# Four seams of a hybrid encoder block in another order on VectorE, ScalarE and GpSimd

## What is computed

```
h = rmsnorm(x, g_mix); z = h @ w_in          # 1024 x 1792: lx, lg, q, k, v
y_lru = rmsnorm(rg_lru(conv(lx)) * gelu(lg), g_lru_out)     # recurrence, 512 channels
y_att = rmsnorm(chunk_window_attention(q, k, v, sinks), g_attn_out)   # 8 heads
x = x + concat([y_lru, y_att]) @ w_out
h = rmsnorm(x, g_ffn)
x = x + square(relu(h @ w_ff1)) @ w_ff2      # hidden width 4096
gate = sigmoid(rmsnorm(x, g_ple) @ w_ple_gate)
x = x + gate * (p @ w_ple_proj)
out = rmsnorm(x, g_final)
```

## Time and profile before

| | us |
|---|---|
| median of 3 runs (1131.03 to 1132.39) | 1131.92 |
| the profiled execution's own time | 1131.98 |
| its span, first to last instruction | 1130.2 |
| PE busy | 1081.9 (96%) |
| DVE busy | 742.2 (66%) |
| POOL busy | 519.3 (46%) |
| ACT busy | 435.3 (39%) |
| granted clock of TensorE, mean | 0.989 |

### The profile page before, as it was taken

The page is one execution under the profiler, slowest core; times in us unless marked ns, Lnnn a source line. Parts: engine busy times, 40 slices in busy tenths (PEclk is TensorE's granted clock), DMA queues, the critical chain, the costliest instruction groups (busy, mean ns, idle before and its releaser), DMA issues.

```text
span 1130.2 us, 13954 instructions
## 1 busy us (share of the span) xinstructions
PE 1081.9 (96%) x5016; PEld 880.7 (78%) x5016; DVE 742.2 (66%) x930; ACT 435.3 (39%) x749; POOL 519.3 (46%) x328
## 2 busy tenths in 40 slices
PE   7999999899989999999999999999999999899996
PEld 5778887676866788888888888888888888678995
DVE  6988639788789846536546545545654653885786
ACT  8554655454446123222222312312311322565455
POOL 2644262232205346256255344444534625565884
PEclk9999999899999999999999999999999999999998
DMA  7211102111001111210211111112111111412352
GB/s 280 75 38 38 38 1 85 38 38 38 1 1 38 54 59 38 74 37 37 74 37 37 74 37 68 44 37 74 37 47 64 37 74 50 173 38 75 111 166 98
DMA packets 22483, 69.45 MB, mean 61 GB/s; under 512 B 2352, under 2 KB 4400, under 8 KB 22448
## 3 DMA queue, kind: packets, MB, share of 16 engines
q1 hardware_dynamic: 22448, 68.99, 17.3%
HBM read 64.79 MB, written 4.19 MB: 61 GB/s over the span
## 4 chain that ended last, share of the span: by engine, by line
PE 77%; DVE 13%; ACT 4%; issue 4%; POOL 2%; DMA 1%; SPq 0%; DVEq 0%; ACTq 0%
PE bank L540 25%; PE bank L541 25%; PE bank L542 25%; DVE xT L1635 1%; DVE r_mix L1246 1%; DVE lane L1293 1%; POOL w_lo L426 1%; DVE acc L325 1%; POOL gx_lo L455 1%; DMA stage<-in_w_in 1%; PE bank L660 1%; PE bank L588 1%; DVE r_ffn L1246 1%; PE bank L630 1%; DVE pT_lo L1673 1%
## 5 line engine op out<-in xcount | busy, mean ns | idle before, releaser
L540 PE MATMUL bank<-h_hi,w_hi 128*128 128x512 f32 (+1 forms) x756 | 291.2, 385 | 18.3 <-DVE h_lo L1233 8.0
L542 PE MATMUL bank<-h_hi,w_lo 128*128 128x512 f32 (+1 forms) x756 | 284.2, 376 | 0.0
L541 PE MATMUL bank<-h_lo,w_hi 128*128 128x512 f32 (+1 forms) x756 | 284.2, 376 | 0.0
L1635 DVE TENSOR_TENSOR xT<-bank,xT 128x512 f32<-128x512 f32 x256 | 173.6, 688 | 114.1 <-PE bank L542 112.3
L540 PE MATMUL bank<-u_hi,w_hi 128*128 128x512 f32 x512 | 202.9, 396 | 7.5 <-DVE xT L1635 6.3
L542 PE MATMUL bank<-u_hi,w_lo 128*128 128x512 f32 x512 | 199.5, 390 | 0.0
L541 PE MATMUL bank<-u_lo,w_hi 128*128 128x512 f32 x512 | 199.4, 389 | 0.0
L540 PEld LDWEIGHTS bank<-h_hi,w_hi 128*128 128x128 f32 x756 | 145.0, 192 | 52.0 <-issue 13.9
L503 POOL TENSOR_TENSOR w_lo<-w_raw,w_hi 128x1024 fp32r<-128x1024 f32 x30 | 78.1, 2626 | 193.2 <-ACT w_hi L1120 193.2
L541 PEld LDWEIGHTS bank<-h_lo,w_hi 128*128 128x128 f32 x756 | 145.0, 192 | 26.1 <-issue 1.9
L542 PEld LDWEIGHTS bank<-h_hi,w_lo 128*128 128x128 f32 x756 | 144.6, 191 | 25.5
(11 more groups left out here) (202 smaller groups left out, 1717.2 us busy)
## 6 DMA issues: line engine op xcount, KB each, us to landing
w_raw<-in_w_ff SPq DMA_DIRECT2D x60, 512.0 KB, 3.6
stage<-in_w_ple_gate SPq DMA_DIRECT2D x24, 512.0 KB, 3.3
stage<-in_w_in SPq DMA_DIRECT2D x13, 512.0 KB, 3.5
stage<-in_w_out SPq DMA_DIRECT2D x8, 512.0 KB, 3.4
xT<-in_x SPq DMA_DIRECT2D x7, 512.0 KB, 9.0
stage<-in_w_ff SPq DMA_DIRECT2D x4, 512.0 KB, 3.2
out_x<-o_ring SPq DMA_DIRECT2D x4, 512.0 KB, 4.2
out_x<-o_ring SPq DMA_DIRECT2D x7, 256.0 KB, 2.2
```

What stands on the lines that cost most here:

```text
L540: pe.matmul(o, whi, hh, start=first, stop=False, skip_group_check=onto)
L541: pe.matmul(o, whi, hl, start=False, stop=False, skip_group_check=onto)
L542: return pe.matmul(o, wlo, hh, start=False, stop=last, skip_group_check=onto)
L1635: dve.tensor_tensor(dst, bank[4 + q % 4][:, :], dst, ALU.add).then_inc(y_added, 1)
```

## The change

No instruction is added or removed but for the place in the queue; one subtraction of weights (`low(2 * FF_FIRST + 3)`) moves from VectorE to GpSimd. The seams:

1. Recurrence norm: both `invert(SS_LRU..)` and both `norm_y` now stand at groups 22 to 24; `softmax_front(1)` stands ahead of `softmax_sum(0)`. ScalarE rounds piece 8 of the weights at unit 1 instead of ahead of unit 0.
2. End of attention: the sums of units 5 to 7 and two of the four multiplications of the attention norm's half 0 come after unit 7's copy of `probT`; PE's `sum_rows(SS_ATT + 1)` comes a group later, `add_a(1)` ahead of `invert`.
3. Start of the feed-forward: the root for half 1 comes between two roundings; `ffn_pair` of half 1 run in one piece, ahead of `rectify` and `hidden_low`; VectorE's `w_low` for one half of piece 12 comes ahead of the reciprocal, and the other half goes to GpSimd. PE's `sum_rows(SS_FFN + 1)` comes one k earlier.
4. End of the feed-forward: `embedding_high` follows the block's last two roundings, `sums(SS_PLE)` on GpSimd and `ple_high` on ScalarE stand ahead of the gate's first weight piece, and `pT_lo`, `pw_lo` come two adds later.

```diff
@@ gpsimd @@
+            low(2 * FF_FIRST + 3)
             pool.wait_ge(w_split, 2 * FF_FIRST + 4)
...
             w2_low(FF_BLOCKS - 1)
+            sums(SS_PLE, sq2, acc2)
             low(2 * GATE_FIRST)
             low(2 * GATE_FIRST + 1)
-            sums(SS_PLE, sq2, acc2)
@@ tensor @@
-                if g == 0:
+                if g == 1:
                     sum_rows(SS_ATT + 1, acc, 5)
...
-                    if hf == 0 and m == 1 and k == 3:
+                    if hf == 0 and m == 1 and k == 2:
                         sum_rows(SS_FFN + 1, acc, 7)
@@ scalar @@
             lru_high(1)
-            piece_free(act, 6)
-            high(2 * 8)
-            high(2 * 8 + 1)
...
+                if u == 1:
+                    piece_free(act, 6)
+                    high(2 * 8)
+                    high(2 * 8 + 1)
...
             high(2 * FF_FIRST + 2)
+            root(SS_FFN + 1, 7, r_ffn, D)
             high(2 * FF_FIRST + 3)
-            root(SS_FFN + 1, 7, r_ffn, D)
-            for k in range(4):
+            for k in range(KD):
                 ffn_split(k, 1)
...
             rectify(1)
-            for k in range(4, KD):
-                ffn_split(k, 1)
...
+                hidden_high(b, 2, late[:, 0, :])
+                hidden_high(b, 3, late[:, 1, :])
                 if last:
                     embedding_high()
-                hidden_high(b, 2, late[:, 0, :])
-                hidden_high(b, 3, late[:, 1, :])
...
-            gate_high(GATE_FIRST)
             for k in range(KD):
                 ple_high(k, 0)
+            gate_high(GATE_FIRST)
@@ vector @@
+                if g == 22:
+                    invert(SS_LRU, r_lru)
+                if g == 23:
+                    norm_y(0)
+                    invert(SS_LRU + 1, r_lru)
                 if g == 24:
-                    invert(SS_LRU, r_lru)
-                    norm_y(0)
+                    norm_y(1)
...
             softmax_front(0)
-            invert(SS_LRU + 1, r_lru)
+            softmax_front(1)
             softmax_sum(0)
-            softmax_front(1)
-            norm_y(1)
...
                 if u == 7:
+                    att_norm(0, (2, 3))
                     att_low(0)
                 add_l(2 * u + 1)
-                if u >= 1:
+                if 1 <= u < 6:
                     unit_sum(u - 1)
                 if u == 6:
-                    att_norm(0)
+                    att_norm(0, (0, 1))
             read_o(UNITS - 1)
-            unit_sum(UNITS - 1)
+            for u in (5, 6, 7):
+                unit_sum(u)
...
             add_a(0)
+            add_a(1)
             invert(SS_ATT + 1, r_mix)
-            add_a(1)
...
             ffn_pair(6, 0)
+            w_low(2 * FF_FIRST + 2)
             invert(SS_FFN + 1, r_ffn)
-            ffn_pair(0, 1)
-            ffn_pair(2, 1)
+            for k in range(0, KD, 2):
+                ffn_pair(k, 1)
...
             hidden_low(1)
-            ffn_pair(4, 1)
-            ffn_pair(6, 1)
-            w_low(2 * FF_FIRST + 2)
-            w_low(2 * FF_FIRST + 3)
...
-                if q < 4:
-                    k, hf = q % 2, q // 2
+                if 2 <= q < 6:
+                    k, hf = q % 2, q // 2 - 1
...
-                elif q < 6:
+                elif q in (6, 7):
```

## The result

| | median of the runs | profiled execution |
|---|---|---|
| before | 1131.72 us | 1131.98 us, span 1130.2 |
| after | 1114.21 us (1113.38 to 1114.94) | span 1113.2 us |

The ratio is 0.9848, 95% interval 0.9835 to 0.986: 17.5 us faster. The direction was right, the gain was undersized by 5.5 us. One execution of the last experiment, y, took 1195.17 us at a mean granted clock of 0.849 and is left out of the ratios; all the others belong to the faster state.

What follows compares the result with a forecast made beforehand. PE, busy 96% of the span, was taken to bound the kernel, so only its waits at the seams could pay. 5.3 + 2.0 + 4.7 = 12.0 us off 1131.98 gave 1120.0 us, own range 1117.5 to 1122.5, wider 1115.0 to 1124.5.

Steps and rivals of the forecast that it cites:

- some 29 us: All seams: PE's waits, lost block time and low-clock stretches together were put at some 29 us.
- Seam 1, 5.3 us: Into the attention: low_y freed from GpSimd's subtractions, probs(2) earlier; 5.3 us gained, bounds 3 and 7.5.
- Seam 2, 2.1 us: End of attention: unit 7's wait and low clock end, PE waits 1.6 us for squares; 2.1 us, bounds 1 and 3.6.
- only 1.3 us earlier: End of attention: GpSimd's third square for the next norm starts only 1.3 us earlier, its reciprocal waiting for PE's sum.
- The 3.6 us for the seam by itself: End of attention: gain of about 3.6 us before PE's 1.6 us wait for the squares cuts it to 2.1.
- Seam 3, -0.1 us net: Into the feed-forward: half 1 ends 7 us earlier, mostly lost in block 0; with seam 2 net 2.0 us.
- beside GpSimd such a step takes 1.70 us: Block 0: VectorE's two-input steps take 1.70 us, not 0.6; first add ends at 351.8, PE waits 5.0 us.
- Rival A: First product, block 0: low clock delays the load past both hidden_low, first add 348.6, 2.6 us more; 1116.5, chance 0.20.
- The 0.7 us booked for a fall of the clock: Block 0: a 5 us wait brings the low clock, PE absorbs most, 0.7 us lost.
- The rule of the Trainium skill: VectorE and GpSimd share an exclusive port lock: 1.89 us a step, 2.1 us more over block 1's weights; rival chance 0.05.
- Seam 4, 4.7 us: End of the feed-forward: 7.3 us gained less a new 2.6 us wait for the scaled gate; 4.7 us, bounds 2 and 7.
- The 7.3 us of block 15: Last feed-forward block: PE never waits, so from start to start of what follows it is 7.3 us less.

Runs made afterwards that it cites:

- y: Changed kernel with probs(2) ahead of GpSimd's weight pair, a gate subtraction behind four squares, ScalarE's root ahead, load held until five groups, block 0 reordered: 1109.12 us.
- s2: Kernel before with only the edits of seam 2, the end of attention: 1128.07 us, ratio 0.9971.
- s3: Kernel before with only the edits of seam 3, into the feed-forward: 1127.86 us, ratio 0.9974.
- s4: Kernel before with only the edits of seam 4, the end of the feed-forward: 1124.34 us, ratio 0.9945.
- d2: Changed kernel with two more VectorE subtractions, their result overwritten, between the second hidden_low and the eight t_make: 1117.07 us, ratio 0.9878.
- x3a: Changed kernel with the feed-forward norm's second root ahead of a ScalarE rounding and VectorE's matching subtraction behind the last pair: 1113.14 us, ratio 0.9838.
- x4: Changed kernel with GpSimd subtracting the second half of the gate's second weight piece behind the first four squares of half 1: 1113.19 us, ratio 0.9842.
- x3b: Changed kernel with the second root and matching subtraction moved as in x3a, and block 1's weight load held until three groups are done: 1112.37 us, ratio 0.9831.

## Why the prediction was wrong, step by step

- **What bounds the kernel.** Right: only where PE stands still did the change pay, and the middle stayed as it was (the gain between block 1 and block 15 is constant at 11.9 us). The "some 29 us" add up to 31.8 from the terms given; nothing was worked out from them.
- **Seam 1, 5.3 us.** Right. `low_y` takes 4.14 us (4.3 forecast), the copy of `probT` starts at 196.72, the moved pair delays `probs(2)` to 209.81 (209.6 forecast), PE waits 1.32 us (1.7):
```profile
192.05 4.14 DVE L1231 TENSOR_TENSOR h_lo<-lane,h_hi 128x512 fp32r<-128x512 f32 x4 [0.19 <-ACT h_hi L870]
...
196.72 0.67 DVE L1476 COPY probT<-bank 128x512 f32<-128x512 f32 x1
...
211.75 1.09 PE L646 MATMUL bank<-ident,prob 128*128 128x128 f32 x8 [1.32 <-POOL prob L436]
```
 Measured 5.7. The 0.4 us to the forecast are no more than what the clock does in that wait by itself (0.4 to 0.8 us in s2, s3 and s4).
- **Seam 2, 2.1 us.** The term that was off is GpSimd's start with the squares: "only 1.3 us earlier". The wait ahead of `h_lo` (0.62 us, 0.7 forecast) and the end of the wait in unit 7 came as said. But before, a square of GpSimd had held up VectorE once among the four multiplications of half 1 and once among the four subtractions (L1231) that make the rests. Before, and after:
```profile
279.18 3.77 DVE L1444 SCALAR_TENSOR_TENSOR qT<-qT,vec,r_mix 128x512 f32<-128x512 f32 x4
...
283.48 3.58 DVE L1231 TENSOR_TENSOR h_lo<-qT,h_hi 128x512 fp32r<-128x512 f32 x4
...
272.89 3.30 DVE L1448 SCALAR_TENSOR_TENSOR qT<-qT,vec,r_mix 128x512 f32<-128x512 f32 x4
...
276.71 2.48 DVE L1231 TENSOR_TENSOR h_lo<-qT,h_hi 128x512 fp32r<-128x512 f32 x4
...
277.53 2.83 POOL L325 TENSOR_TENSOR acc<-acc,sq 128x512 f32<-128x512 f32 x1 [3.88 <-ACT sq L877]
...
280.54 5.60 POOL L325 TENSOR_TENSOR acc<-acc,sq 128x512 f32<-128x512 f32 x4 [0.18 <-ACT sq L877]
...
286.56 1.28 POOL L325 TENSOR_TENSOR acc<-acc,sq 128x512 f32<-128x512 f32 x1 [0.42 <-ACT sq L877]
```
 The multiplications took 3.77 us and now 3.30 (the first of them still met a square), the subtractions 3.58 and now 2.48; GpSimd waited instead (2.83 us for 1.29). The four squares in a row began at 288.41 and now at 280.54; less seam 1's 5.2 that is 2.7 us earlier, and PE's wait for their sum was 0.09 us. The 3.6 us for the seam by itself are 3.0 by the terms given (2.0 + 1.7 - 0.7); without the wait taken off, 3.2 were measured. It is akin to the mistake in block 0: I moved VectorE's operations as they were, with their stalls.
- **Seam 3, -0.1 us net.** Wrong, and the larger half of the miss, for 3.0 us were gained. The reciprocal, the end of half 1 and GpSimd's start were each within 1.2 us of the forecast. The step that failed is "beside GpSimd such a step takes 1.70 us [...], not 0.6. So the first add ends at 351.8". The steps ahead of the first add took 0.60 us each in after, d2, x3a and x4, and in after that add ended at 342.04 (347.2 on the clock of before, 4.6 us ahead of the forecast). In after itself two things kept GpSimd behind both `hidden_low`: VectorE was 1.3 us earlier, mostly by seam 2, and the clock's fall held the load back 1.5 us, as in Rival A. But x4, without that fall and with GpSimd ahead of both, gained the same 11.9 us, so it is the price that failed. Rival A had the better time, 348.6, and its condition came true in after, yet the gain did not hang on it. The 0.7 us booked for a fall of the clock "behind the 5 us wait" were not lost either, since the longest wait there was 1.10 us.
- **The rule of the Trainium skill**, named in the prediction ("SBUF — State Buffer", section "SBUF: two separate sides": an exclusive lock, held for the whole instruction) agrees with what is seen: GpSimd's 4.03 us in x4 are 2.75 of standing and 1.28 of work, and it did not slow VectorE meanwhile. By the page I made the price larger, 1.89 us a step; the runs show it smaller. The lock agrees; what counted was the order of turns, and of that the price says nothing.
- **Seam 4, 4.7 us.** The 7.3 us of block 15 were right (7.2), as was a wait for the gate at the third group. The wait was 1.24 us, not 2.6. GpSimd's four subtractions took 11.28 us, and the squares of half 1 began at 991.06, as forecast (1002.8 on the clock of before is 991.4 here). From there to the root it was 6.75 us, not 7.9, and the reciprocal followed 1.1 us ahead of the forecast. I had the reciprocal follow the root by one `split_low`, and the root follow GpSimd; x4 shows that an earlier root brings no earlier reciprocal, which stands behind VectorE's own `split_low`. The squares began here:
```profile
979.83 11.28 POOL L426 TENSOR_TENSOR w_lo<-stage,w_hi 128x1024 fp32r<-128x1024 f32 x4
...
991.06 1.08 POOL L323 COPY acc<-sq 128x512 f32<-128x512 f32 x1
```
- **The sum.** 0.4 + 1.1 + 3.1 + 1.0 = 5.6 us, all to one side. 4.2 us of it are seams 2 and 3: collisions of VectorE and GpSimd that I carried over or priced in, and the 0.7 us for the clock.
- **Range.** The bounds of the seams had been 7.5, 3.6 and 7; for seam 3 there was no bound on the good side but rival A. Rival A's 2.6 us, seam 2's upper bound (1.5 more) and seam 4's (2.3 more) together give 1113.6. As all three hang on how VectorE and GpSimd meet, they had to be added and not set against one another.

## What to carry to other kernels

The cost of VectorE beside GpSimd is that of a pattern and not of an instruction: read it from rows with the same neighbours, and price a run of two-input steps both ways, beside the other engine and at its lone time. Where two engines take turns, add up both their work over the stretch; shifting one operation within it bought nothing (x4), holding one engine back until the other's first adds were through did (x3b). Give every seam its own range, since errors of one reading go the same way in all of them.

## What the runs showed of the hardware

Whether a wait is followed by a fall of TensorE's clock is not settled by its length: at the same place of the same code 1.84 us (after) were followed by 3.41 us at 1.2 GHz and 1.85 us (x4) by none, and at one place in the gate 2.26 us (up to 1077.19) were followed by a fall in after, and 2.29 us by none in x3b and in y. The row of x4 from the first product to its end shows the clock at 1.00:
```profile
321.00:334.00 13.00, 11.18 (x48) 8.95 (x49) 10.94 (x17) 8.55 (x15) 0.00 (x0) 1.00 0.01 4
```
Between traces of the same work this moves a place by up to 0.8 us (first column of s2, s3 and s4).

GpSimd, released from idle in block 0, was kept out by VectorE for up to 2.75 us (x4), as long as VectorE's steps with two SBUF inputs followed at once. It isn't always so. In seam 4 seven `split_low` in a row, which also have two SBUF inputs, took 12.92 us and the last four of them 1.70 us each, in strict turns with a GpSimd that was at work when they began. And at 284.30 before, a square released 0.22 us into a subtraction went in behind it and held the next one to 1.78 us, while at 277.53 after, released equally 0.22 us into one, it stood until the last. What decides who is next stays open; no run here tells it.
